# Routing's gated one-hot rows made on ScalarE alone, as rectified gate minus gate times distance

## What is computed

```python
def peer(xf, w_query, sub_keys_a, sub_keys_b, expert_u, expert_v):
    qry = (xf @ w_query).reshape(T, PEER_HEADS, 2, PEER_DKEY // 2)
    sa = jnp.einsum('thd,nd->thn', qry[:, :, 0], sub_keys_a)
    sb = jnp.einsum('thd,nd->thn', qry[:, :, 1], sub_keys_b)
    va, ia = lax.top_k(sa, PEER_TOPK)
    vb, ib = lax.top_k(sb, PEER_TOPK)
    ...
    top_s, pos = lax.top_k(cand, PEER_TOPK)
    experts = jnp.take_along_axis(cand_idx, pos, axis=-1)
    gates = jax.nn.softmax(top_s.astype(jnp.float32), axis=-1)
    ...
        act = jax.nn.gelu(jnp.einsum('tkd,td->tk', expert_u[eb], xb), approximate=False)
        return jnp.einsum('tk,tkd->td', gb * act, expert_v[eb])
```

## Time and profile before

| | |
|---|---|
| runs (3) | median 3937.39 us, 3934.48 to 3939.39 |
| profiled execution | 3936.05 us |
| its span in the profile | 3934.3 us |
| busy in the span | PE 3475.2, DVE 2792.3, POOL 1469.0, ACT 925.7 us |
| routing's gated turns | from about 1523 to 1986 us of the span |
| `apply` | from 1995 us to the end |
| granted TensorE clock, mean | 0.925 |

### The profile page before, as it was taken

How to read it: one execution, slowest core, us unless ns; L and a number is a source line. 1 busy time by engine, 2 the same in 40 slices (tenths; PEclk the granted TensorE clock), 3 DMA queues, 4 the chain that set the end, 5 groups by cost and what they waited for, 6 DMA issues and landing times. The chain is left out here.

```text
span 3934.3 us, 39919 instructions
## 1 busy us (share of the span) xinstructions
PE 3475.2 (88%) x13263; PEld 1956.9 (50%) x13263; DVE 2792.3 (71%) x5246; ACT 925.7 (24%) x1903; POOL 1469.0 (37%) x1284
## 2 busy tenths in 40 slices
PE   7677999978888858896579999999999999999995
PEld 2443554335555558886434444444444444444442
DVE  1352457764566537888948889789897888877777
ACT  0052210004566402554521111111111111111110
POOL 1210004650000000000027666567656677676664
PEclk9787999986889879998689999999999999999998
DMA  9654325982111155754279999999999999899997
GB/s 345 253 212 141 121 86 219 376 312 108 46 43 38 19 189 201 260 202 163 86 293 360 377 387 378 354 391 386 379 369 378 391 392 381 341 405 390 383 369 258
DMA packets 350974, 1060.51 MB, mean 270 GB/s; under 512 B 31616, under 2 KB 90288, under 8 KB 344880
## 3 DMA queue, kind: packets, MB, share of 16 engines
q0 software_dynamic: 175936, 664.89, 44.2%
q1 hardware_dynamic: 174832, 393.05, 27.5%
HBM read 992.26 MB, written 65.31 MB: 269 GB/s over the span
## 5 line engine op out<-in xcount | busy, mean ns | idle before, releaser
L2788 PE MATMUL psH<-XT,e_uT 128*128 128x512 f32 x2048 | 930.9, 596 | 7.5 <-ACT e_uT L2825 7.5
L2801 PE MATMUL psY<-e_v,e_W 128*128 128x512 f32 x2048 | 881.5, 592 | 0.0
L2736 POOL DMA_INDIRECT pick_u<-in_expert_u,ids x512 | 669.7, 1308 | 386.0 <-DVE pick_dot L2902 272.8
L2918 DVE SCALAR_TENSOR_TENSOR acc<-pick_v,pick_w,acc 128x1024 f32<-128x1024 f32 x508 | 652.4, 1284 | 172.5 <-DMA pick_v<-in_expert_v,ids 130.9
L2744 POOL DMA_INDIRECT pick_v<-in_expert_v,ids x512 | 573.9, 1121 | 238.1 <-issue 146.0
L2902 DVE CUSTOM_DVE_ANT_0 e_junk<-pick_u,x_rows 128x1024 bf16<-128x1024 f32 x512 | 624.5, 1220 | 22.5 <-DMA pick_u<-in_expert_u,ids 10.6
L2801 PEld LDWEIGHTS psY<-e_v,e_W 128*128 128x128 f32 x2048 | 389.1, 190 | 489.8 <-issue 489.3
L2788 PEld LDWEIGHTS psH<-XT,e_uT 128*128 128x128 f32 x2048 | 370.8, 191 | 379.7 <-issue 369.2
L781 PE MATMUL ps_p<-w_in_sb,hT 128*128 128x512 f32 x896 | 393.7, 599 | 9.5 <-ACT stage L896 9.5
L2825 ACT ACTIVATE e_uT<-psU 128x512 f32<-128x512 f32 x256 | 152.1, 596 | 714.7 <-PE psU L2780 635.6
L781 PEld LDWEIGHTS ps_p<-w_in_sb,hT 128*128 128x128 f32 x896 | 170.8, 192 | 218.5 <-issue 208.1
(11 more groups left out here) (578 smaller groups left out, 4141.4 us busy)
## 6 DMA issues: line engine op xcount, KB each, us to landing
w_query_sb<-in_w_query SPq DMA_DIRECT2D x32, 2048.0 KB, 8.3
e_u<-in_expert_u SPq DMA_DIRECT2D x128, 512.0 KB
e_v<-in_expert_v SPq DMA_DIRECT2D x128, 512.0 KB
G_d<-G_stage SPq DMA_DIRECT2D x16, 2048.0 KB, 11.6
e_g<-G_d SPq DMA_DIRECT2D x16, 2048.0 KB
w_ada<-in_w_ada POOLq DMA_DIRECT2D x16, 1024.0 KB, 14.0
h_w_in<-in_w_in SPq DMA_DIRECT2D x7, 2048.0 KB, 15.5
w_in_sb<-in_w_in SPq DMA_DIRECT2D x7, 2048.0 KB, 16.6
```

Of the source, the lines that this page charges most:

```text
L2736: pool.indirect_dma_start(gu[:, i % NGU, :], None, io["expert_u"][0], bass.IndirectOffsetOnAxis(ids[:, q % 2, j:j + 1], 0)).then_inc(pu_in ...
L2788: m = pe.matmul(psH[a % 2][:, :], uT[:, a % 2, j, :], XT[:, j, :], start=j == 0, stop=j == KD - 1)
L2801: m = pe.matmul(psY[i % NY][:, :], W[:, (b * NBK + t) % NW, k * P:(k + 1) * P], v[:, t, half_cols(half)], start=t == 0, stop=t == NBK - 1)
L2918: dve.scalar_tensor_tensor(out=sums_q, in0=gv[:, i % NGV, :], scalar=wgt[:, m % 2, o:o + 1], in1=sums_q, op0=ALU.mult, op1=ALU.add).then_i ...
```

## The change

The plain one-hot rows of side a are no longer made. For a pick with number a and gate g, ScalarE computes for n = 0 to 127

first |a - n|, with `number` as the input, scale -1 and the column a as the bias, and then max(0, g - g * |a - n|), with the column -g (the new tile `gates_less`) as the scale and the column g as the bias.

It is g where n = a, and max(0, g - g * k) = 0 for the distances k = 1, 2, ... elsewhere. `gate_a` becomes `gated_a`: eight Abs operations, a drain, eight Relu operations. It waits for kT_set and for a free buffer of the ring instead of VectorE's rows. VectorE's `hot` makes `ob` alone; `keep_picks` also negates the gates, and its signal moves behind the drain.

```diff
--- before.py
+++ after.py
@@ -2299,7 +2299,7 @@
         number, number_i = sb("number", [P, NK]), sb("number_i", [P, NK], I32)
         ab = sb("ab", [P, 2, KX])
         ssq, rstd = sb("r_ssq", [P, 1]), sb("r_rstd", [P, 1])
-        kT = sb("kT", [P, 2, 3, P])
+        kT, less = sb("kT", [P, 2, 3, P]), sb("gates_less", [P, 2, P])
         oa, ob = sb("hot_a", [P, NO, GT, NK]), sb("hot_b", [P, NO, GT, NK])
         gs = sb("G_stage", [P, NS_, NK, HT])
         psT, psQ, psS, psG = ps("r_psT", [P, D]), ps("r_psQ", [P, 512]), ps("r_psS", [P, 512]), ps("psG", [P, 2, GT, NK])
@@ -2310,7 +2310,7 @@
         q_out, q_copied, sc_out, sc_copied = sem("q_out"), sem("q_copied"), sem("sc_out"), sem("sc_copied")
         soft_v, soft_a, made, made_t, kT_set = sem("soft_v"), sem("soft_a"), sem("made"), sem("made_t"), sem("kT_set")
         hf_kept, sg_kept = sem("hf_kept"), sem("sg_kept")
-        oa_hot, oa_set, ob_set, g_out, g_kept = sem("oa_hot"), sem("oa_set"), sem("ob_set"), sem("g_out"), sem("g_kept")
+        oa_set, ob_set, g_out, g_kept = sem("oa_set"), sem("ob_set"), sem("g_out"), sem("g_kept")
         g_stored = [sem(f"g_stored{i}") for i in range(NS_)]
         block = ctx.enter_context(nc.Block())
 
@@ -2488,10 +2488,17 @@
                     act.wait_ge(sg_kept, 16 * nth_kept[k])
                 act.activation(scores(k)[:, 4 * g:4 * g + 4, :], psS[:, :].rearrange("p (j t) -> p j t", t=P), ACT.Copy).then_inc(sc_copied, 1)
 
-            def gate_a(i, d, n):
-                act.wait_ge(oa_hot, i + 1)
+            def gated_a(i, d, n):
+
+                of = lambda which, t: kT[:, d % 2, which, n * GT + t:n * GT + t + 1]
+                act.wait_ge(kT_set, d + 1)
+                if i >= NO:
+                    act.wait_ge(g_out, i - NO + 1)
                 for t in range(GT):
-                    m = act.activation(oa[:, i % NO, t, :], oa[:, i % NO, t, :], ACT.Copy, scale=kT[:, d % 2, 2, n * GT + t:n * GT + t + 1])
+                    act.activation(oa[:, i % NO, t, :], number[:, :], ACT.Abs, scale=-1.0, bias=of(0, t))
+                act.drain()
+                for t in range(GT):
+                    m = act.activation(oa[:, i % NO, t, :], oa[:, i % NO, t, :], ACT.Relu, scale=less[:, d % 2, n * GT + t:n * GT + t + 1], bias=of(2, t))
                 m.then_inc(oa_set, 1)
 
             def keep(i):
@@ -2510,7 +2517,7 @@
                         if at == 0:
                             norm(i)
                     if j >= 1:
-                        gate_a((j - 1) * SLOTS + s, j - 1, s)
+                        gated_a((j - 1) * SLOTS + s, j - 1, s)
                         if s >= 1:
                             keep((j - 1) * SLOTS + s - 1)
                     for i, k, at in in_turn(j, s):
@@ -2560,16 +2567,17 @@
 
             def keep_picks(d):
                 dve.wait_ge(made_t, d + 1)
-                dve.tensor_copy(kT[:, d % 2, :, :], psT[:, 0:3 * P].rearrange("p (j t) -> p j t", t=P)).then_inc(kT_set, 1)
-                dve.drain()
+                dve.tensor_copy(kT[:, d % 2, :, :], psT[:, 0:3 * P].rearrange("p (j t) -> p j t", t=P))
+                dve.tensor_scalar(less[:, d % 2, :], psT[:, 2 * P:3 * P], -1.0, None, ALU.mult)
+                dve.drain()
+                dve.sem_inc(kT_set, 1)
 
             def hot(i, d, n):
                 at = slice(n * GT, (n + 1) * GT)
                 if i >= NO:
                     dve.wait_ge(g_out, i - NO + 1)
-                for which, o, done in ((0, oa, oa_hot), (1, ob, ob_set)):
-                    dve.tensor_tensor(o[:, i % NO, :, :], number[:, :].unsqueeze(1).broadcast_to([P, GT, NK]),
-                                      kT[:, d % 2, which, at].unsqueeze(2).broadcast_to([P, GT, NK]), ALU.is_equal).then_inc(done, 1)
+                dve.tensor_tensor(ob[:, i % NO, :, :], number[:, :].unsqueeze(1).broadcast_to([P, GT, NK]),
+                                  kT[:, d % 2, 1, at].unsqueeze(2).broadcast_to([P, GT, NK]), ALU.is_equal).then_inc(ob_set, 1)
 
             def split():
 
```

## The result

| | before | after |
|---|---|---|
| median, beside each other on one chip | 3935.93 us (3930.04 to 3939.39, 4 runs) | 3993.32 us (3980.45 to 3995.72, 4 runs) |
| ratio, 95% interval | 1 | 1.0146 [1.0121, 1.0171] |
| profiled execution, span | 3936.05, 3934.3 | 3980.45, 3978.7 |
| first gated operation of ScalarE to the end of the last copy of psG | 1533.40 to 1986.46: 453.1 us | 1520.41 to 2027.30: 506.9 us |

The change costs 57 us by the medians. The forecast was 32 us more, 3969 us, and the range ended at 3993, which the median passes by 0.3 us: the sign is right, the size is short by almost half.

A forecast was written before the change was run, and what follows sets the result against it. VectorE was taken to bound routing's gated turns, with ScalarE setting the pace after the change. 28 us from ScalarE's sum plus 4 for TensorE's clock, on 3937.39, gave 3969 us, 0.8% slower, range 3942 to 3993.

The forecast's parts named there:

- What bounds before: Routing's gated turns: VectorE sets the pace of the chain VectorE to ScalarE to TensorE; at most 72 us to gain.
- ScalarE's block: Eight gated rows on ScalarE: Abs 2.44, drain 0.07, Relu 3.07, together 5.58 us; a slot takes 6.4 us.
- VectorE does not come later: Gated slots: VectorE does not set the pace but idles, some 50 us for the norm, 40 to 50 for psG.
- The cover that the working called thin at three places: Turn starts: ScalarE's first two blocks behind the norm, 11.3 us, cover 9.6 us of VectorE work queued behind it.
- The waits for queries: ScalarE waiting for TensorE's queries: 41 us in all, plus 5.5 us for the turns' last products.
- TensorE's clock: Products behind 3.6 us pauses: one or two of twelve fall to a low clock, 4 us, bounds 0 and 35.
- rival 4: TensorE's clock falls in most of the twelve places: 28 + 35 us, 4000 us (3985 to 4002), chance 0.13.
- The sum: ScalarE's slots, small copies and waits added from 1533.4 us: routing ends at 2014.2 against 1986.46, 28 us later.
- The signs: Profile marks expected after the change; wrong if, among others, the first three turns do not each grow 7 to 12 us.
- Busy times: Engine busy times after the change: ScalarE's up by about 245 us, VectorE's down by 77.
- Rival 1 and 2: Column operands cheaper, Relu pass 2.44 us: 3942 us, chance 0.12; ScalarE's block short enough to win: 3912 us, chance 0.07.
- Rival 3: VectorE stays the bound in routing and all 72 us are gained: 3865 us, chance 0.03.

The follow-up runs named there:

- e1: Changed kernel without ScalarE's Abs pass and drain, second pass a plain copy times the gate (table wrong), against the kernel before: 3885.44 us, ratio 0.9871.
- e5: Changed kernel with VectorE again making its eight plain side-a rows per slot, into an unread scratch tile: 3993.3 us, ratio 1.0138 to the kernel before.
- e6: Changed kernel with 8 overwritten identity products on TensorE in each slot without queries: 3959.39 us, ratio 1.0067 to the kernel before.
- e3: Changed kernel with the Relu pass at constant scale -1 instead of the negated-gate column: 3954.12 us, ratio 1.0056 to the kernel before.
- v3: Changed kernel with rows shared between VectorE and ScalarE by a per-slot table, Relu scale -1, plus 8 identity products in slots without queries: 3902.80 us.
- e7: The changed kernel run again without any edit, for a second trace: 3985.99 us, ratio 1.0125 to the kernel before.

## Why the prediction was right in sign and short in size

- **What bounds before: right.** e1 shows it: with VectorE relieved and ScalarE as before, the kernel gains 49 us. The 72 us called the most that can be had are not reached even so.
- **ScalarE's block: right, a little short.** Abs is 390 ns and 2.44 us a pass, as taken. The Relu pass is 3.18 us against 3.07, its pitch (3.18 - 0.48)/7 = 0.386 us against 0.37. A slot without queries is 6.50 us from start to start (6.4), so 64 slots are 6 us more; with the small copies this part of the sum is 9 us larger (506.9 less its waits of 63.6 is 443.3, against 434.3). The Trainium skill (ScalarE: Activation LUTs, What ACT_TABLE_LOAD costs) had the better number with its 93 ns for each column operand: the trace has 92 ns between 480 and 388, and the pass of 3.18 us that was estimated from it is the one measured. The row of hT, 454 ns from PSUM, was too cheap a neighbour even with the 0.02 us added.
- **VectorE does not come later: right for the slots, not for the starts of turns.** Its waits are 59.7 us for the norm (some 50 foreseen, the longest 17.4 where 10 to 15 was said) and 60.9 for psG (40 to 50), and e5 puts 74 us of work into them for 6 us of time. The cover that the working called thin at three places did not hold there: TensorE waits 1.03, 1.27 and 0.99 us for VectorE's copy of the turned rows.
- **The waits for queries, the clock aside: a little high.** e6, where the clock holds, has 39.3 us of waits on ScalarE in the stretch; the sum had 41 + 5.5. The first groups of turns 2 and 3 wait 2.9 and 2.6 us, where 1.3 + 2.9 was taken. The 2.9 were the price of a product at the low clock there, and in the changed kernel that product takes 2.05 to 2.09 us; the wait has another cause, of which 1.27 and 0.99 us are TensorE's wait for VectorE's copy. These groups are the larger part of what the sum had too much. The block's 9 us more and these 7 less all but cancel, and e6's stretch is 482.5 - 453.1 = 29.4 us longer: the 28 of the sum.
- **TensorE's clock: the step that failed.** I wrote "I take one or two of the twelve: 4 us", with no row for that count. All twelve were slow, in both profiles of the changed kernel, and what it costs is 506.9 - 482.5 = 24 us. The size of one fall was overrated in turn, 2.9 us, taken from a first group: ScalarE's waits for queries at the twelve places are 36.3 us in the changed kernel and 14.9 in e6, 21.4 for the twelve, some 1.6 us at ten of them and 2.9 and 2.5 at the other two. The last products of the turns make the other 3.2. The count was the mistake. The earlier trace rows showed one product behind a pause of 3.44 us at the low clock, and the working itself had 3.6 us for the pause; both pointed to rival 4, which had the mechanism and, at 35 us, a price half as much again as the true one. The median, 3993, lies in rival 4's 3985 to 4002. Against it stood the granted clock of 0.94 in the first turn of before and the full rate at the twelve places there; but these belong to shorter pauses, and the change lengthens the pause and thins the work on both sides of it.
- **The sum.** 28 + 9 - 7 + 24 = 54 us, against 53.8 measured on the stretch.
- **The signs.** The last one named, that the prediction is wrong if the first three turns do not each grow by 7 to 12 us, came true: they grew by 17.3, 19.1 and 13.8. The turns of e6 grew by 8.8, 8.3 and 10.1, so it is the clock that took them out of the band.
- **Busy times.** ScalarE's grew by 200 us, not the 245 I wrote: the old pass was 156.3 us for 512, the new ones are 155.8 + 204.0, so the difference is the second pass alone. The block's own numbers, 64 times 5.58 less 2.44, give 201, and nothing in the working stands behind the 245. VectorE's fell by 71 (77 said). Neither number carries the sum.
- **The rivals.** Rival 1 and 2 fall by the group's 480 ns. Rival 3, that VectorE stays the bound, falls by the waits. e3 shows what rival 1's price would have been: at 388 ns the kernel takes 3954 us, not the 3942 of the working; seven of its twelve products are still slow, so a part of the clock's cost is in it.

## What to carry to other kernels

Before work is moved to an engine because it stands idle, add up its block: here 202 us were to go into 167 us of waiting, and a share of the work, a different one for each slot, brought 32 us where all of it cost 57. Where a change lengthens the pauses of TensorE, look up in the trace what a product behind a pause of the new length takes, and price the case that all of them are like it; then ask who waits for TensorE there. A test of it is cheap: let it multiply something into a buffer that is overwritten anyway, and see whether the time falls. Such a filling helps only where the pause is long enough to hold it: with pauses of 0.34 us in the kernel before, and in v3, it delayed the queries behind it.

## What the runs showed of the hardware

- In the changed kernel products behind pauses of 2.71, 3.27 and 3.59 us alike met the low clock (2.64 to 3.79 us instead of 1.95 to 2.05), between slots in which TensorE had a product and little more. The length of the pause does not settle it alone: in e3 products behind 2.85 us took 2.05 at two places and 2.53 to 3.48 at six, and one behind 1.98 us took 3.17; in e5 two of the twelve took 2.05 behind the full 3.59, one of them this:

```profile
1589.83 2.05 PE L2438 MATMUL psG<-hot_a,hot_b 128*128 128x128 f32 x16 [3.59 <-ACT hot_a L2501]
```

- Filling 1.95 us of the pause was enough for the full rate at all twelve places of e6, with 0.94 to 1.81 us of it left idle; filling all of it raised the granted clock further, 0.93 to 0.98, and brought no more time.
- Sixteen instructions took 3.79, 3.45, 2.81 or 2.64 us at different places with pauses of nearly the same length. The level is not tied to the start of the work. Around the product of 2.64 us, which starts at 1776.32 us, the granted clock is 1.00 through the pause and the product's first 1.26 us, and falls in its middle:

```profile
1776.32:1777.58 1.26, 1.26 (x11) 1.00 1.05 393
1777.58:1778.96 1.38, 1.38 (x9) 0.51 0.51 189
```

- In e7 other places had the long waits (3.87 us in turn 3, 2.78 where the first profile had 4.31). A single place is no measure of it, the stretch is.
- Executions of one kernel differ by 10 us and more in code that the kernels share: ScalarE's first gated operation began at 1520.4, 1529.3, 1533.4 and 1537.5 us in the profiles of the changed kernel, of its repetition, of before and of e6. What causes it was not looked into.
- The drain between the two passes is 0.07 us (1687.37 + 2.44 to 1689.88), as in the norm; 4.5 us for all 64.
